# One decoder step on one core: the expert loop turned so that both branches come before the scatter, numbering after the second branch, placing ahead of the second token turn, activation turns as transposes

## The chip, the cores and the metric

The kernel runs on one core of a Trainium2 chip. The metric is device time in microseconds (us), the median of three runs. Durations and times within the program come from one profiled execution. An operand is always float32 unless said otherwise.

## The reference

One inference step of a one-layer decoder trunk for 256 prompt tokens and 32 sample tokens, 288 in all, of width 2048: a mixing block, cross-attention, and a hierarchical mixture of experts, which is where the change lies. For the normed tokens `t` it computes

```python
p_g = softmax(t @ wg + bg); g_sel = argmax(p_g)            # one of 4 groups
e_sel = (t @ we + be) of that group                        # 4 experts in it
top_p, top_i = top_k(softmax(e_sel), 2)
wts = top_p / sum(top_p) * p_g[g_sel]
act = silu(t @ w_gate[e]) * (t @ w_up[e]) * gate           # per chosen expert, d_ff = 512
out = act @ w_down[e]
x = x + out;  y = rmsnorm(x, norm_final)
```

There are 16 experts, each with w_gate and w_up of 2048 x 512 and w_down of 512 x 2048.

## The kernel before, in words

The engines run programs of their own and meet by semaphores: PE multiplies, ACT (ScalarE), DVE (VectorE) and POOL (GpSimd) do the rest, and SP issues the loads. The program is written out by hand, so the order in the code is the order on each engine. PE's results lie in PSUM in eight banks of 512 columns.

**Work of the expert stage.** A job is one expert with up to C = 64 tokens, its slots. Jobs go in pairs, and `n_loops` pairs run in a loop that all engines have, with one pair more behind it. The trace has eight pairs: seven turns and the last. Each pair takes 24 weight tiles of 1 MB (2048 columns on 128 partitions), numbered from `TILE["moe"]`: 0 to 7 gate and up of the first job, 8 to 15 gate and up of the second, 16 to 23 down of both. For the loop's own numbers 24 to 39 are the branches of the next pair. They go through 14 slots (`moe_slot`), and SP issues them in that order (`moe_load`, L596 to L612), each when PE has released the tile that lay in its slot: tiles 14 to 23 lie where 2 to 11 of the same pair lay, and 26 to 35 where 14 to 23 lay; slots 0, 1, 12 and 13 are used once in a pair. An issue that waits holds back all behind it.

**Work of a pair on PE.** `pair` (L1194) begins when the first job's branch is done:
- `place` (L1176): six small products and turns from `pick` (which token sits in which slot), for the gates and the matrix `spread` that takes slots back to tokens;
- `turn_act` (L1184): the activated branch of job 0 is turned, as four products with the identity;
- `branch(1, 8, ...)` (L1162): job 1's gate and up products, four groups of two tiles each, into one bank, `BRANCH_BANK`. Behind its first group stands `number_slots` (L1153), which works out the slots of the next pair;
- a second `turn_act`, which waits for ACT's silu (L1537) and DVE's product (L2133) of that branch;
- the down products (L1220) into banks 4 to 7, four groups of two tiles;
- ACT and DVE copy the result, scaled, to `y_pair` (L1552, L2146); then the scatter (L1230), 16 products of `y_pair` with `spread` in four steps of four, each of which DVE adds to the residual `xT` (L2152);
- in a loop turn `branch(0, 24, ...)`: job 0's branch of the next pair, behind the last addition.

POOL gathers the tokens of the next pair into `xe` (`gather`, L739): job 0's slots once their numbers are there and PE is through with the old ones, then job 1's. DVE makes the next pair's `pick` (`make_picks`, L2106).

**Ahead of the loop.** The routing works on all 288 tokens in three chunks: 128, 128 and the 32 of the sample. PE turns the normed tokens to rows (L1103), ACT scales them (`tokens_out`, L1486), PE turns them back (`turn_back`, L1112), ACT copies them to `h_moe` (L1496, L1500). Behind all three turns, PE counts for every token its place in its expert's queue (L1146), DVE makes `pick` from it (L2066 to L2074), and PE numbers the slots (L1157); ACT copies these (L1517). Then POOL gathers the first 32 slots of each job of pair 0, and ACT the other 32 (L1527), and PE starts `branch(0, 0, None)`, the first of 64 rows at L1170. Only then does the loop come.

Of the kernel before, what the change touches and what calls it, by code (L numbers as in the profile page):

```python
# [13 lines left out]
P = 128  # L14
D = 2048
DB = D // P
TP = 256
# [43 lines left out]
PE_EVENTS, MOE_SLOTS = 7, 14  # L61
HC = C // 2
NX = NJ - NE
# [17 lines left out]
for _n, _c in (("x", 1), ("pack", 1), ("h", 3), ("x_rest", 2), ("mem", 2), ("gates", 4), ("mix_stat", 2),  # L81
               ("states", 1), ("xattn_stat", 2), ("router", 1), ("h_tok", 1), ("logits", 1), ("h_tok_rest", 2),
               ("h_moe", 3), ("places", 1), ("counts", 1), ("pick_0", 1), ("moe", 6), ("final_sum", 1), ("y_0", 1), ("final_stat", 1), ("y_rest", 2)):
# [51 lines left out]
def build(nc, a, o):  # L135
    ctx = ExitStack()
    with ctx:
# [26 lines left out]
        expert_of = sb("expert_of", [1, NJ], I32)  # L164
# [5 lines left out]
        def cut(at, *shape):  # L170
# [55 lines left out]
        job_first, at = cut(at, NJ)  # L226
# [85 lines left out]
        xe_ready, xe_second_half = sem("xe_ready"), sem("xe_second_half")  # L312
        h_tok_out, h_moe_out, root_loaded = sem("h_tok_out"), sem("h_moe_out"), sem("root_loaded")
        place_out, act_out, product_out, low_banks_out, high_banks_out = map(
            sem, ("place_out", "act_out", "product_out", "low_banks_out", "high_banks_out"))
# [126 lines left out]
        slot_sums = ps[0:1, 7, 3 * P:3 * P + 2 * C]  # L442
        place_sums = lambda c: bank(UNIT["places"], 1 + c // 2)[:, c % 2 * P:c % 2 * P + NE]
        first_slot_sums = ps[0:1, 4 * ((UNIT["places"] + 1) % 2) + 3, 0:2 * C]
# [209 lines left out]
        def _(pool):  # L654
# [84 lines left out]
            def gather(p, s, slots):  # L739

                for first in range(0, slots, 16):
                    at = C * s + first
                    for n, token in enumerate(tokens_of_slots(mybir.EngineType.Pool, p, at, 16)):
                        m = nc.gpsimd.tensor_copy(xe[:, :, at + n:at + n + 1], h_moe_or_zero[:, :, bass.ds(token, 1)])  # L744
# [5 lines left out]
            for s in range(2):  # L750
                gather(0, s, HC)
# [11 lines left out]
        def _(pe):  # L763
# [369 lines left out]
            for c in range(2):  # L1133
                start_unit(pe, UNIT["h_moe"] + c)
                turn_back(c, lambda b: bank(UNIT["h_moe"] + c, b // 4)[:, b % 4 * P:(b % 4 + 1) * P])
# [24 lines left out]
            ACT_BANK, BRANCH_BANK, GATE_BANK, SPREAD_BANK = 4, 5, 6, 7  # L1160

            def branch(s, t, i, groups=range(4)):  # L1162

                for g in groups:
                    wait_moe_tile(pe, t + 2 * g, i)
                    wait_moe_tile(pe, t + 2 * g + 1, i)
                    for k in range(KT):
                        b = KT * g + k
                        for n in range(2):
                            m = mm(ps[C * n:C * n + C, BRANCH_BANK, :], xe[:, b, C * s:C * s + C],  # L1170
# [4 lines left out]
            def place():  # L1175

                for c in range(3):
                    n = own_rows[c]
                    mm(ps[:, GATE_BANK, 0:2], pick[0:n, c, :], job_gate[0:n, c, :], start=(c == 0), stop=(c == 2))
                for c in range(3):  # L1180
                    n = own_rows[c]
                    nc.tensor.transpose(ps[:, SPREAD_BANK, c * P:c * P + n], pick[0:n, c, :], ident[0:n, 0:n])
# [8 lines left out]
            def scatter_bank(q):  # L1191

                return 4 * ((q + 1) % 2)

            def pair(i, last):

                place()
                pe.wait_ge(product_out, plus(1, i, 2))
                turn_act()
                pe.wait_ge(xe_ready, plus(2, i, 2))  # L1200
                branch(1, 8, i, range(1))
                if not last:
                    pe.wait_ge(pick_ready, plus(2, i, 1))
                    pe.wait_ge(place_out, plus(1, i, 1))
                    number_slots(slot_sums)
                branch(1, 8, i, range(1, 4))
                pe.wait_ge(product_out, plus(2, i, 2))
                pe.wait_ge(act_out, plus(1, i, 2))
                turn_act()

                if not last:
                    pe.wait_ge(slots_out, plus(2, i, 1))
                pe.wait_ge(act_out, plus(2, i, 2))
                pe.wait_ge(place_out, plus(1, i, 1))
                for k in range(KT):
                    for s in range(2):
                        wait_moe_tile(pe, 16 + 2 * k + s, i)
                    for b in range(4):
                        for s in range(2):
                            m = mm(ps[C * s:C * s + C, 4 + b, :], actT[:, s, k, :],  # L1220
                                   moe_tile(16 + 2 * k + s)[:, b * TW:(b + 1) * TW], start=(k == 0), stop=(k == KT - 1))
                    m.then_inc(tile_used, 2)
                for q in range(4):
                    if q % 2 == 0:
                        pe.wait_ge(high_banks_out, plus(2 + q // 2, i, 4))
                    elif q == 3:
                        pe.wait_ge(low_banks_out, plus(1, i, 2))
                    for b in range(4):
                        j = 4 * q + b
                        m = mm(ps[:, scatter_bank(q) + b, 0:T], y_pair[:, j * P:(j + 1) * P], spread[:, :],  # L1230
                               start=True, stop=True)
                    m.then_inc(unit_done, 1)
                if not last:
                    pe.wait_ge(low_banks_out, plus(2, i, 2))
                    pe.wait_ge(high_banks_out, plus(4, i, 4))
                    pe.wait_ge(xe_ready, plus(3, i, 2))
                    branch(0, 24, i)
# [975 lines left out]
```

## Time and profile before

| | |
|---|---|
| median of three runs | 1531.19 us |
| the three runs | 1523.59, 1531.19, 1532.20 us |
| profiled execution, its own time | 1530.45 us |
| its span | 1528.7 us |
| granted TensorE clock, mean | 0.978 of full |
| PE busy | 1431.7 us, 94% of the span |
| DVE, ACT, POOL busy | 36%, 12%, 52% |
| bytes by DMA | 377.07 MB, 247 GB/s mean |

The span runs from the first to the last instruction; the execution's own time is 1.75 us longer. Busy PE time holds pipelined products whose ends are modelled. A clock of 1.00 in a stretch is 2.4 GHz, 0.50 is 1.2 GHz. A float32 product shows as two PE rows, so that the 32 products of one group of two tiles, at 512 columns and two at a time, are 16 rows in the chain.

### The profile page before, as it was taken

How to read it: one execution, taken by the hardware profiler on the slowest of the kernel's cores; microseconds unless marked ns; L12 is line 12 of the kernel's file. 1: busy time of each engine (PE TensorE's matmuls, PEld its weight loads, DVE VectorE, ACT ScalarE, POOL GpSimd, SP SyncE). 2: the span in 40 equal slices, each digit the busy share in tenths (PEclk: the TensorE clock that was granted, in tenths of full speed). 3: DMA queues.
4: the chain of work that ended last, by engine and by line, in shares of the span. 5: the costliest groups of instructions: out<-in, count | busy, mean ns of one | idle time of the engine just before them, and what ended most of it. 6: DMA issues, size and time to landing. Idle time of an engine off the chain costs nothing.

```text
span 1528.7 us, 25461 instructions
## 1 busy us (share of the span) xinstructions
PE 1431.7 (94%) x9302; PEld 1113.5 (73%) x9302; DVE 555.8 (36%) x1018; ACT 187.6 (12%) x390; POOL 797.3 (52%) x1461
## 2 busy tenths in 40 slices
PE   7999999999989999999999899979989999899997
PEld 6999999998879999987777699943443434434434
DVE  3546578749573423112111631231211112212104
ACT  4101321000000010013222100060000000000002
POOL 3777598879967757753453547324053151340500
PEclk8999999999999999999999899979999999999999
DMA  7344344445544444555879434829999999999991
GB/s 248 121 155 145 103 138 142 161 162 182 179 153 158 156 146 140 218 194 189 306 305 359 140 111 165 327 114 384 420 414 417 404 423 404 422 404 403 422 371 62
DMA packets 106121, 377.07 MB, mean 247 GB/s; under 512 B 12422, under 2 KB 12422, under 8 KB 76291
## 3 DMA queue, kind: packets, MB, share of 16 engines
q1 hardware_dynamic: 103778, 371.68, 64.3%
q10 hardware_dynamic: 2272, 4.42, 0.8%
q8 instruction: 48, 0.79, 0.2%
q14 instruction: 23, 0.18, 0.0%
HBM read 369.30 MB, written 6.77 MB: 246 GB/s over the span
## 4 chain that ended last, share of the span: by engine, by line
PE 89%; DVE 5%; ACT 2%; issue 1%; DMA 1%; SPq 0%; POOL 0%; POOLq 0%; ACTq 0%; DVEq 0%
PE ps L835 39%; PE ps L1170 15%; PE ps L892 13%; PE ps L1220 8%; PE ps L1230 4%; PE ps L960 2%; PE ps L785 1%; PE ps L1187 1%; PE ps L978 1%; DVE xT L2152 1%; PE ps L968 1%; PE ps L1026 1%; DVE A L2146 1%; PE ps L999 0%; DMA A<-in_norm_final 0%
## 5 line engine op out<-in xcount | busy, mean ns | idle before, releaser
L835 PE MATMUL ps<-hT,tiles 128*128 128x144 f32 x1792 | 295.3, 288 | 8.2 <-ACT kv_stage L1397 3.2
L744 POOL COPY A<-A 128x16 f32 x960 | 146.6, 212 | 299.5 <-issue 299.5
L835 PE MATMUL ps<-A,tiles 128*128 128x144 f32 x1792 | 265.2, 288 | 5.8 <-DVE mT L1643 3.9
L835 PEld LDWEIGHTS ps<-hT,tiles 128*128 128x128 f32 x1792 | 251.5, 191 | 9.9 <-ACT kv_stage L1397 3.5
L835 PEld LDWEIGHTS ps<-A,tiles 128*128 128x128 f32 x1792 | 239.9, 192 | 6.9 <-issue 4.7
L699 POOL TENSOR_TENSOR tiles<-tiles 128x512 f32<-128x512 f32 x88 | 117.4, 1334 | 192.1 <-DMA tiles<-in_w_in 70.2
L835 PE MATMUL ps<-tiles 128*128 128x144 f32 x960 | 170.9, 287 | 0.0
L1170 PE MATMUL ps<-tiles,A 128*64 128x512 f32 x512 | 146.8, 606 | 20.1 <-DVE xT L2152 12.7
L835 PEld LDWEIGHTS ps<-tiles 128*128 128x128 f32 x960 | 140.2, 191 | 0.0
L892 PE MATMUL ps<-tiles,mT 128*128 128x256 f32 x512 | 132.8, 382 | 4.1 <-ACT kv_stage L1397 4.1
L1662 DVE COPY pair_sums<-ps 128x144 f32<-128x144 f32 x44 | 13.5, 308 | 312.5 <-PE ps L835 312.5
L704 POOL TENSOR_TENSOR tiles<-tiles 128x512 f32<-128x512 f32 x88 | 119.1, 1354 | 6.9
L702 POOL TENSOR_TENSOR tiles<-tiles 128x512 f32<-128x512 f32 x88 | 121.7, 1383 | 0.0
L701 POOL TENSOR_TENSOR tiles<-tiles 128x512 f32<-128x512 f32 x88 | 117.6, 1336 | 6.9
L1220 PE MATMUL ps<-tiles,mT 128*64 128x512 f32 x448 | 120.1, 614 | 0.0
L892 PEld LDWEIGHTS ps<-tiles,mT 128*128 128x128 f32 x512 | 93.6, 190 | 23.0 <-ACT kv_stage L1397 6.8
L1170 PEld LDWEIGHTS ps<-tiles,A 128*64 128x64 f32 x512 | 45.6, 139 | 85.1 <-issue 84.6
L892 PE MATMUL ps<-tiles,A 128*128 128x256 f32 x384 | 103.8, 379 | 0.0
L689 POOL TENSOR_TENSOR tiles<-tiles 128x512 f32<-128x512 f32 x32 | 45.4, 1418 | 100.6 <-DMA tiles<-in_xa_w_v 90.6
L2133 DVE TENSOR_TENSOR mT<-mT,ps 64x512 f32<-64x512 f32 x16 | 11.0, 690 | 228.4 <-ACT mT L1537 228.4
L1170 PE MATMUL ps<-A 128*64 128x512 f32 x320 | 87.2, 599 | 0.0
L892 PEld LDWEIGHTS ps<-tiles,A 128*128 128x128 f32 x384 | 73.0, 190 | 9.9
(341 smaller groups left out, 1708.1 us busy)
## 6 DMA issues: line engine op xcount, KB each, us to landing
tiles<-in_expert_w_down SPq DMA_DIRECT2D x56, 1024.0 KB, 8.6
tiles<-in_w_in SPq DMA_DIRECT2D x40, 1024.0 KB, 5.1
tiles<-in_expert_w_gate SPq DMA_DIRECT2D x32, 1024.0 KB, 11.1
tiles<-in_expert_w_up SPq DMA_DIRECT2D x32, 1024.0 KB, 12.0
A<-in_expert_w_up SPq DMA_DIRECT2D x24, 1024.0 KB, 12.5
tiles<-in_xa_w_k SPq DMA_DIRECT2D x16, 1024.0 KB, 5.1
tiles<-in_w_out SPq DMA_DIRECT2D x16, 1024.0 KB, 5.1
tiles<-in_xa_w_q SPq DMA_DIRECT2D x16, 1024.0 KB, 5.0
```

Source lines behind the costliest of these rows:

```text
L689: step.tick(tt(t1, b12, b11, ALU.subtract))
L699: step.tick(tt(s1, a21, a22, ALU.add))
L701: tt(a21, a11, a21, ALU.subtract)
L702: step.tick(tt(s2, s1, a11, ALU.subtract))
L704: tt(s4, a12, s2, ALU.subtract).then_inc(weights_summed, 1)
L744: m = nc.gpsimd.tensor_copy(xe[:, :, at + n:at + n + 1], h_moe_or_zero[:, :, bass.ds(token, 1)])
L835: return mm(one(u + mp, x, TH), w[:, kp, mp, :], rhs, start=(first and g == 0 and kp == 0), stop=(g == 3 and kp == 1), skip_group_check=True)
L892: return mm(one(u, x, TW // 2), own, w[:, kp, :], start=(first and g == 0 and kp == 0), stop=(g == 3 and kp == 1), skip_group_check=True)
L960: m = nc.tensor.transpose(attention_bank(i % 2)[:, b * P:(b + 1) * P], cache_tile(tile)[:, (4 * (i % 4) + b) * P:(4 * (i % 4) + b + 1) * P ...
L1170: m = mm(ps[C * n:C * n + C, BRANCH_BANK, :], xe[:, b, C * s:C * s + C], moe_tile(t + 2 * g + n).rearrange("p (k n) -> p k n", k=KT)[:, k, :],
L1220: m = mm(ps[C * s:C * s + C, 4 + b, :], actT[:, s, k, :], moe_tile(16 + 2 * k + s)[:, b * TW:(b + 1) * TW], start=(k == 0), stop=(k == KT ...
L1230: m = mm(ps[:, scatter_bank(q) + b, 0:T], y_pair[:, j * P:(j + 1) * P], spread[:, :], start=True, stop=True)
```

## The change

On PE the loop is turned. Ahead of it now stand the whole first pair of branches; a turn is `down(i)`, `branch(0, 24, i)` and `second_branch(32, 4, i, True)`: `place`, branch 1 of the next pair, and behind that branch the numbering of the pair after it and the scatter of pair i. The scatter is eight steps of two products, each added by DVE on its own, in two alternating pairs of banks; four steps stand ahead of the second activation turn and four behind it. The two branches get banks of their own (4 and 5), down uses banks 0 to 3, and the activation turn bank 7. `make_picks` runs one pair further ahead, so the tables `expert_of` and `job_first` have two entries more. Three of the four products of an activation turn become transposes.

Ahead of the loop the places are worked out behind the first turn back, and DVE computes the gates after `pick` and no longer before. The first gather is split 24 : 24 : 16 between POOL, ACT and DVE, for job 0; job 1 keeps 32 : 32.

In the diff, cut to what the text speaks of:

```diff
-               ("values", 8), ("heads", 2), ("w_o", 8), ("router", 1), ("h_tok", 3), ("h_moe", 2),
-               ("places", 1), ("final_stat", 1), ("y", 3)):
+               ("values", 8), ("heads", 2), ("w_o", 8), ("router", 1), ("h_tok", 3), ("h_moe", 1),
+               ("places", 1), ("h_moe_rest", 1), ("final_stat", 1), ("y", 3)):
...
-            for s in range(2):
-                gather(0, s, HC)
+            gather(0, 0, POOL_SLOTS)
+            gather(0, 1, HC)
...
+            turn_back_chunk(0, UNIT["h_moe"])
             u = UNIT["places"]
             start_unit(pe, u)
-            turn_back(2, lambda b: bank(u, 0)[:, b * NB * ST:(b + 1) * NB * ST])
...
             def turn_act():
 
                 for k in range(KT):
-                    m = mm(ps[:, ACT_BANK, k * C:(k + 1) * C], act_nat[0:C, k * P:(k + 1) * P], ident[0:C, 0:C],
-                           start=True, stop=True)
+                    dst, own = ps[:, ACT_BANK, k * C:(k + 1) * C], act_nat[0:C, k * P:(k + 1) * P]
+                    if k == 0:
+                        mm(dst, own, ident[0:C, 0:C], start=True, stop=True)
+                    else:
+                        m = nc.tensor.transpose(dst, own, ident[0:C, 0:C])
                 m.then_inc(unit_done, 1)
...
+            def scatter(u, i):
+
+                if u < 2:
+                    pe.wait_ge((y_low_out, y_high_out)[u], plus(1, i, 1))
+                    pe.wait_ge(place_out, plus(1, i, 1))
+                else:
+                    pe.wait_ge(residual_added, plus(8 + u - 1, i, 8))
+                for n in range(2):
+                    j = 2 * u + n
+                    m = mm(ps[:, 2 * (u % 2) + n, 0:T], y_pair[:, j * P:(j + 1) * P], spread[:, :], start=True, stop=True)
+                m.then_inc(unit_done, 1)
+
+            def second_branch(t, n, i, scattered):
+
+                pe.wait_ge(xe_ready, plus(n, i, 2))
                 place()
+                branch(1, t, i, range(1))
+                pe.wait_ge(product_out, plus(n - 1, i, 2))
+                turn_act()
+                branch(1, t, i, range(1, 4))
+                pe.wait_ge(pick_ready, plus(n // 2 + 1, i, 1))
+                number_slots(slot_sums)
+                if scattered:
+                    for u in range(4):
+                        scatter(u, i)
+                pe.wait_ge(product_out, plus(n, i, 2))
+                pe.wait_ge(act_out, plus(n - 1, i, 2))
+                turn_act()
+                if scattered:
+                    for u in range(4, 8):
+                        scatter(u, i)
...
+            second_branch(8, 2, None, False)
             with pe.Fori(0, n_loops) as i:
-                pair(i, False)
-            pair(n_loops, True)
+                down(i)
+                pe.wait_ge(xe_ready, plus(3, i, 2))
+                branch(0, 24, i)
+                pe.wait_ge(place_out, plus(1, i, 1))
+                second_branch(32, 4, i, True)
+            down(n_loops)
...
             with dve.Fori(0, n_loops) as i:
                 step.enter(i, 2)
-                pair(i, False)
+                e = EVENT["moe"]
+                upper_y(i)
+                product(24, 0, 3, i)
+                turned_act(0, e, i)
+                make_picks(i + 2)
+                product(32, 1, 4, i)
+                for u in range(4):
+                    add_scattered(u, e + 2 + u, i)
+                turned_act(1, e + 6, i)
+                for u in range(4, 8):
+                    add_scattered(u, e + 3 + u, i)
```

How this moves the instructions is shown at three places. The names in the rows are tiles in SBUF and PSUM: `ps` is PSUM, `A` holds `xe`, `y_pair`, `pick` and some weight tiles, `mT` the activations, and `tiles`, `kv_stage` and `hT` hold weight tiles. A name behind "waits" is a semaphore.

PE in the loop, from the end of the second job's branch to the down products (L1220), in the kernel before:

```order
L1170 MATMUL ps<-A 64x512 [waits moe_loaded3,moe_loaded2]
L1170 MATMUL ps<-A 64x512 x7
L1187 MATMUL ps<-ident,mT 128x64 [waits act_out,product_out]
L1187 MATMUL ps<-ident,mT 128x64 x3
L1220 MATMUL ps<-kv_stage,mT 64x512 [waits moe_loaded4,place_out,moe_loaded5,act_out,slots_out]
```

The same place now, where L1160 is the numbering, L1206 the scatter and L1192 with L1194 the activation turn:

```order
L1173 MATMUL ps<-A 64x512 x7
L1217 REGISTER_ALU
L1160 MATMUL ps<-A 1x128 [waits pick_ready]
L1160 MATMUL ps<-A 1x128 x2
L1206 MATMUL ps<-A 128x288 [waits place_out,y_low_out]
L1206 MATMUL ps<-A 128x288
L1206 MATMUL ps<-A 128x288 [waits place_out,y_high_out]
L1206 MATMUL ps<-A 128x288
L1203 REGISTER_ALU
L1206 MATMUL ps<-A 128x288 [waits residual_added]
L1206 MATMUL ps<-A 128x288
L1203 REGISTER_ALU
```

The second activation turn stood directly behind the branch whose product it waits for; now the numbering and four scatter steps stand between the two, and four steps more behind the turn.

PE in the loop, from the end of the down products to the next pair's first branch, before:

```order
L1220 MATMUL ps<-tiles,mT 64x512 x7
L1225 ISA
L1230 MATMUL ps<-A 128x288 [waits high_banks_out]
L1230 MATMUL ps<-A 128x288 x7
L1225 REGISTER_ALU
L1230 MATMUL ps<-A 128x288 [waits high_banks_out]
L1230 MATMUL ps<-A 128x288 x3
L1230 MATMUL ps<-A 128x288 [waits low_banks_out]
L1230 MATMUL ps<-A 128x288 x3
L1235 REGISTER_ALU [waits low_banks_out]
L1236 REGISTER_ALU [waits high_banks_out]
L440 REGISTER_ALU [waits xe_ready]
```

And now, with the down products at L1239 and the branch at L1173:

```order
L1239 MATMUL ps<-tiles,mT 64x512 x7
L1261 REGISTER_ALU
L442 ISA [waits xe_ready]
L1173 MATMUL ps<-tiles,A 64x512 [waits moe_loaded1,moe_loaded0]
L1173 MATMUL ps<-A 64x512
```

The branch no longer stands behind the copies to `y_pair`, the scatter and the additions; it waits for the gathered tokens and its tiles alone.

ACT ahead of the loop, from the last `tokens_out` to the copy of the slot numbers, before:

```order
L1486 ACTIVATE mT<-ps,mT 32x2048 [waits unit_done]
L1496 COPY A<-ps 128x16x128 [waits half0_free,unit_done]
L1496 COPY A<-ps 128x16x128 [waits half1_free,unit_done]
L1500 COPY A<-ps 128x16x32 [waits half0_free,unit_done]
L1517 CAST tiles<-ps 1x128 [waits unit_done]
```

And now, with `tokens_out` at L1510, the turned-back chunks at L1517 and L1539, the exponentials at L1533 and the slot numbers at L1525:

```order
L1510 ACTIVATE mT<-ps,mT 32x2048 [waits half1_free,unit_done]
L1517 COPY A<-ps 128x16x128 [waits half0_free,unit_done]
L1533 ACT_TABLE_LOAD [waits half1_free]
L1533 ACTIVATE mT<-mT 128x3x4 [waits gate_in]
L1534 ACTIVATE mT<-mT 128x3
L1517 COPY A<-ps 128x16x128 [waits unit_done]
L1525 CAST tiles<-ps 1x128 [waits half1_free,unit_done]
L1539 COPY A<-ps 128x16x32 [waits unit_done]
```

The slot numbers stand ahead of the sample's copy instead of behind it, and the exponentials between the two chunks.

## Rows read from the trace of the kernel before

**Rows 1.** The page: GB/s moved, in 40 equal slices of the span

```profile
GB/s 248 121 155 145 103 138 142 161 162 182 179 153 158 156 146 140 218 194 189 306 305 359 140 111 165 327 114 384 420 414 417 404 423 404 422 404 403 422 371 62
```

**Rows 2.** The chain that ended last, one pair: start, us, engine, line, count

```profile
1243.03 15.66 PE ps L1220 x64
...
1258.72 1.29 DVE A L2146
...
1260.06 8.04 PE ps L1230 x32
1268.13 1.36 DVE xT L2152
...
1269.91 13.95 PE ps L1170 x64
1283.86 0.85 PE ps L1179 x6
1284.71 0.54 PE ps L1182 x3
1285.27 1.10 PE ps L1187 x8
1286.37 3.58 PE ps L1170 x16
1289.95 0.83 PE ps L1157 x6
1290.79 10.47 PE ps L1170 x48
1301.28 0.60 ACT mT L1537
...
1301.91 0.70 DVE mT L2133
...
1304.32 15.66 PE ps L1220 x64
```

**Rows 3.** The same chain: down products of the second and of the last pair

```profile
1122.17 13.97 PE ps L1220 x64
...
1487.36 13.97 PE ps L1220 x64
```

**Rows 4.** Windows: busy us by engine, then PEclk, DMA share, GB/s

```profile
1243.00:1244.50 1.50, 1.47 (x4) 0.53 (x6) 0.00 (x0) 0.00 (x0) 1.17 (x8) 0.58 1.01 421
...
1206.90:1208.60 1.70, 0.00 (x0) 0.00 (x1) 1.30 (x1) 0.00 (x0) 0.00 (x0) 1.00 1.02 424
```

**Rows 5.** Windows of the weight stream, same columns

```profile
1100.00:1152.00 52.00, 46.81 (x214) 21.55 (x215) 10.89 (x19) 3.26 (x7) 19.56 (x128) 0.97 1.00 417
...
1221.00:1273.00 52.00, 46.81 (x215) 21.43 (x213) 10.88 (x19) 3.26 (x7) 19.54 (x128) 0.97 1.01 423
...
1275.00:1282.00 7.00, 7.00 (x36) 2.82 (x34) 0.00 (x0) 0.00 (x0) 0.00 (x0) 1.00 0.84 316
```

**Rows 6.** SP's issue of the fifteenth tile, and its time to landing

```profile
1033.69 0.35 SPq L612 DMA_DIRECT2D A<-in_expert_w_gate  x1
...
A<-in_expert_w_gate SPq DMA_DIRECT2D x1, 1024.0 KB, 4.9
```

**Rows 7.** Timeline ahead of the loop: PE, ACT, ACT, POOL, PE

```profile
1009.01 1.97 PE L1112 MATMUL ps<-ident,A 128*128 128x128 f32 x16 [0.21 <-ACT mT L1486]
...
1011.17 1.87 ACT L1496 COPY A<-ps 128x2048 f32<-128x2048 f32 x1 [0.17 <-ACT A L1496]
...
1017.40 0.26 ACT L1517 CAST tiles<-ps 1x128 int32<-1x128 f32 x1 [3.66 <-PE ps L1157]
...
1019.21 2.43 POOL L744 COPY A<-A 128x16 f32 x16 [26.79 <-issue]
...
1024.71 1.08 PE L1170 MATMUL ps<-tiles,A 128*64 128x512 f32 x1 [7.34 <-POOL A L744]
```

**Rows 8.** Timeline of DVE in an earlier stage: an addition of 576 columns

```profile
963.45 0.76 DVE L1878 TENSOR_TENSOR xT<-xT,ps 128x576 f32<-128x576 f32 x1
```

More of the change, by code:

```diff
@@ L58 @@
 NSTATE = S_SC + (1 + NB) * (SW - 1)
-PE_EVENTS, MOE_SLOTS = 7, 14
+PE_EVENTS, MOE_SLOTS = 11, 14
 HC = C // 2
+POOL_SLOTS, ACT_SLOTS = 24, 48
 NX = NJ - NE
@@ L1218, in pair @@
                     for b in range(4):
+                        if k == 0 and b % 2 == 0:
+                            pe.wait_ge(residual_added, plus(8 - 1 + b // 2, i, 8))
                         for s in range(2):
-                            m = mm(ps[C * s:C * s + C, 4 + b, :], actT[:, s, k, :],
+                            m = mm(ps[C * s:C * s + C, b, :], actT[:, s, k, :],
                                    moe_tile(16 + 2 * k + s)[:, b * TW:(b + 1) * TW], start=(k == 0), stop=(k == KT - 1))
                     m.then_inc(tile_used, 2)
[L1223 to L1237, printed above, removed]
-            read_out(pe, UNIT["h_moe"] + 1)
+            turn_back_chunk(1, UNIT["h_moe_rest"])
             pe.wait_ge(tokens_numbered, 1)
@@ L1539, in pair, with place_read @@
-            def pair(i, last):
-                e = EVENT["moe"]
+                fn(silu[0:C, :], ps[0:C, 4 + s, :], ACT.Silu).then_inc(silu_ready, 1)
+            def place_read(e, i):
                 after_event(act, e, i, PE_EVENTS)
                 for s in range(2):
-                    copy(place_gate[C * s:C * s + C, 0:1], ps[C * s:C * s + C, 6, s:s + 1])
-                copy(spread[:, :], ps[:, 7, 0:T]).then_inc(place_out, 1)
-                if not last:
-                    slots_numbered(slot_sums, e + 1, i, i + 1)
-                gate_branch(8, i)
+                    copy(place_gate[C * s:C * s + C, 0:1], ps[C * s:C * s + C, 6, T + s:T + s + 1])
+                copy(spread[:, :], ps[:, 6, 0:T]).then_inc(place_out, 1)
@@ L1549, in pair, with lower_y @@
+            def lower_y(i):
                 after_tile(act, TILE["moe"] + 16 + 7, i, 24)
                 act.wait_ge(place_out, plus(1, i, 1))
-                dst, src = lower(y_pair, 4)
-                fn(dst, src, ACT.Copy, scale=place_gate[:, 0:1]).then_inc(high_banks_out, 1)
-                if not last:
-                    gate_branch(24, i)
-            gate_branch(0, None)
+                dst, src = lower(y_pair, 0)
+                fn(dst, src, ACT.Copy, scale=place_gate[:, 0:1]).then_inc(y_low_out, 1)
@@ L2047, in _ @@
             m.then_inc(mask_ready, 1)
+            dve.wait_ge(consts_set, 10)
+            u = UNIT["places"]
+            after_event(dve, EVENT["places"])
+            for c in range(3):
+                m = stt(out=posm[:, c, :], in0=place_sums(c), scalar=4.0 * NOWHERE, in1=mask16[:, c, :],
+                        op0=ALU.add, op1=ALU.mult)
+            then(m)
+            then(ts(posm[:, :, :], posm[:, :, :], -4.0 * NOWHERE, None, ALU.add))
+            for g in range(2):
+                for c in range(3):
+                    m = ts(pick[:, c, C * g:C * g + C], place_iota[:, 0, :], posm[:, c, g:g + 1], None, ALU.is_equal)
+            m.then_inc(pick_ready, 1)
+            after_event(dve, EVENT["counts"])
+            v.tensor_copy(tab[:, 0, :], bank(u, 3)[:, 0:NE]).then_inc(half_free[u % 2], 2)
+            dve.wait_ge(gate_exp, 2)
             then(v.tensor_reduce(G(18, 1), G(4), AX.X, ALU.add))
@@ L2059, in _ @@
             then(m)
-            dve.wait_ge(consts_set, 10)
-            u = UNIT["places"]
-            after_event(dve, EVENT["places"])
-            for c in range(3):
-                m = stt(out=posm[:, c, :], in0=place_sums(c), scalar=4.0 * NOWHERE, in1=mask16[:, c, :],
-                        op0=ALU.add, op1=ALU.mult)
-            then(m)
-            then(ts(posm[:, :, :], posm[:, :, :], -4.0 * NOWHERE, None, ALU.add))
             dve.wait_ge(root_loaded, 1)
@@ new lines, in _ @@
+            step.leave_dynamic(n_loops)
+            upper_y(n_loops)
+            for q in range(4):
+                after_event(dve, EVENT["scatter"] + q, n_loops, PE_EVENTS)
+                first = 4 * ((q + 1) % 2)
+                x = xT[:, 4 * q:4 * q + 4, :]
+                tt(x, x, ps[:, first:first + 4, 0:T], ALU.add).then_inc(last_added, 1)
+                dve.wait_ge(last_added, q + 1)
+                for b in range(4 * q, 4 * q + 4):
+                    m = ts(hT[:, b, :], xT[:, b, :], gain("norm_final", b), None, ALU.mult)
+                m.then_inc(h_ready, 1)
```

201 lines of the change are left out of this document (96 added, 105 removed).

## The prediction

> **What bounds the kernel now.** I read the page's slices first. From the 29th to the 38th they move 403 to 423 GB/s; ahead of that the rate changes from slice to slice [rows 1]. That is the expert stage, which streams its weights. Then the chain that ended last, for one pair. From one start of the down products to the next are 1304.32 - 1243.03 = 61.29 us, and almost all of it is PE: down 15.66, scatter 8.04, first branch 13.95, `place` 0.85 + 0.54, activation turn 1.10 (there are two), second branch 3.58 + 10.47, numbering 0.83 [rows 2]. Between these PE stands still for others: 1.29 for the copy to `y_pair`, 1.36 for the last addition to `xT`, 0.60 + 0.70 for silu and product, and some 1.5 in hand-offs that the rows leave as gaps. So PE is the bound by the chain.
>
> The down products take 15.66 us here and 13.97 in the second and the last pair [rows 2, 3]. The difference, 1.69, is clock: just behind the wait for the product and the short turn, the window from 1243.00 shows 0.58, which is a mixture of 1.2 and 2.4 GHz. But a wait alone didn't do it: the 1.70 us from 1206.90, in which PE is idle after the scatter's last step, stand at 1.00 [rows 4]. The row with 15.66 comes five times, and in one more turn the same time is lost in the first group of the second branch; so six of the seven turns of the loop take 61.3 us, counted between the ends of the down products.
>
> Then the windows of the stream, which decide the case. Over 52 us it moves 423 GB/s in one pair and 417 in an early one; only in the 7 us around 1278 does it fall to 316 [rows 5]. That is a hole of (423 - 316) / 423 x 7 = 1.8 us. A pair's 24 tiles are 24 x 1.0486 = 25.17 MB; at 422, between the two rows and nearer to the one that repeats, they take 59.6 us, 2.485 a tile. 59.6 + 1.8 is the 61.3 of the pair. So the stream is only 1.7 us faster than PE, and the hole is its own waiting for a slot: whoever takes more than 1.7 us a pair from PE makes the stream the bound.
>
> **The change in the loop, PE's side.** PE's work in a turn is down 13.97 at full clock, first branch 13.95, `place` 1.39, second branch 14.05, numbering 0.83, scatter 8.04: 52.2 [rows 2, 3]. Two turns come to it. Three transposes in `place` are three instructions (0.54 x3), where the activation turn's four products are eight, 0.14 each [rows 2]. With one product and three transposes five are left, 0.7 a turn. Bounds: 0.55, if only four issue slots count, and the old 1.10. With 0.6 for hand-offs, PE needs 54.2 us.
>
> The waits go as follows. The copy to `y_pair` (1.29) lies beside the first branch, which now has banks of its own. Silu and product of the first branch (1.3) lie beside `place` and the second branch's first group (5.0). Those of the second lie beside numbering and two scatter steps, 0.83 + 2.0. What is late next there is the first addition: DVE has it behind the product, at 1.4 us after the branch, while scatter step 0 ends at 1.8, so the product doesn't delay it. Each scatter step is 8.04 / 8 = 1.0 us of PE; an addition of 576 columns took 0.76 [rows 8], and step u + 2 waits for addition u with step u + 1 between: 0.8 under 1.0, hidden. POOL's gather now runs beside these additions. If it slowed them to what twice the columns take, 1.36 [rows 2], the chain would be DVE's, 8 x 0.4 = 3 us longer. I take 0, since POOL was at work beside the 0.76 too.
>
> The gather of the next pair starts at the numbering, not in the middle of the branch. 64 slots are four times 2.86 us (2.43 and the loading of 16 numbers), 11.4 us [rows 7]. From the numbering to the next first branch are 9.6 + 13.97 = 23.6 us, so 12 us of cover are left; every us beyond it would stand on PE. The order in which SP issues is the same, no queue gets another DMA, and the two new entries of the tables change no tile.
>
> **The stream's side.** 54.2 is 5.4 below 59.6, so PE catches up and then waits for tiles: 3.49 us of work in a group against 4.97 for its two tiles. From there each pair costs 59.6, not 54.2. Does the stream get a new hole? Tile 26 goes where tile 14 lay. In the first pair PE is through with 14 at some 1054, and the stream reaches 26 at 1063; later, PE uses each tile as it lands, and even behind the scatter's 9.9 us pause only four of 14 slots have filled. I count no hole. Gain: 61.3 - 59.6 = 1.7 in each of six loop turns, 10 us, out of 7.1 that PE saves in each.
>
> **Ahead of the loop.** Before, ACT copied the second chunk until 1013.04, and the slot numbers were out at 1017.66, since places, `pick` and numbering came behind it; ACT idled 3.66 in it [rows 7]. Now these lie beside the chunks. In return the second chunk can be turned only when ACT has emptied the first, near 1011, so PE's 1.97 no longer overlaps: 1013.0, numbering 1013.9, the copy until 1014.9, slot numbers 1015.2, and the sample's copy, with a quarter of the columns 0.5 to 0.6, until 1015.9. With PE at half clock it is 1017. The exponentials, which now stand between the two chunks on ACT, lie beside PE's turn. I take 1016.4, 1.3 earlier. POOL then gathers 24 slots instead of 32 ahead of PE's start: 8 x 2.43 / 16 = 1.2. DVE's 16 copies of the same kind are not in the trace; between 0 and POOL's 2.43 for 16 they are done before POOL's 24, but their numbers must be loaded first, as POOL's were (1.55 from 1017.66 to 1019.21), by an engine that has the gates to finish. Sum 2.5, bounds 0 and 3.5.
>
> **The sum.** The fifteenth tile is issued at 1033.69, when the first branch has freed its slot, and lands 4.9 later, at 1038.6 [rows 6]. Now 2.5 earlier: 1036.1. 177 further tiles at 2.485 land until 1475.9. The last second branch has its tiles eight earlier, at 1456.0. Behind them PE has 3.5 for the group, 0.83, 8.04, 0.7 and 0.3 of hand-offs: 1469.4. Down adds 13.97, its tiles being there: 1483.3. Before it was 1487.36 + 13.97 = 1501.3 [rows 3]: 18 us, made of 2.5 ahead, 10 in the loop and 5.5 in the last pair, where PE is again alone. The end, 1528.7 - 1501.3 = 27.4, is kept in its old form. That gives a span of 1510.7 and, with the 1.75 around it, 1512. The profiled execution had 1530.45 and the median is 1531.19, so the same sum from there ends within 1 us.
>
> **Two rules of the Trainium skill.** PE will idle 1.5 us per group, which no row shows in this rhythm. The Trainium skill, "TensorE: Matmul & The Clock Gate", section "HAM oscillation — how this bites in real kernels", tells of a kernel that waits for a DMA behind each batch of products and is thrown back to the low clock every time. By it each group would be colder, as the second rival has it; the row from 1206.90 speaks against it. And "DMA: Bandwidth & Descriptors" of the Trainium skill, section "Where 436 GB/s comes from", gives 435 GB/s as the ceiling of the fabric and warns of about 358 from HBM. This stream holds 423, so the trace contradicts the lower one. By the upper one a pair would take 57.8, an estimate from that page, and the time would be some 13 us less.
>
> **The rivals.** *The stream stays the bound* (1512): for it the flat 423, a row that comes alike in five turns, and a hole exactly as long as PE's excess. Chance 0.72, with a range of its own from 1506 to 1518.
>
> *PE's new order costs back its slack.* Four stretches at the low clock per turn, each 1.69, make 54.2 + 6.8 = 61.0, so PE is nearly as slow as before; up to three are hidden in the 5.4. Then seven turns cost 1.4 more each: 1522. For it: such a stretch came once in almost every pair. Against: it came where short turns and a wait fell together, and these are now apart. Chance 0.20.
>
> *PE is still the bound and the stream follows*: the first branch starts at 1022.2; it, with 1.69 at the low clock, `place`, the second branch, both turns, numbering, the wait for the product and down are 48.6 us, so the first down ends at 1070.8. With 7 x 54.2, 27.4 and 1.75 that is 1479. For it is only that PE fills the chain; no window of the stream shows the rate of 464 GB/s that it needs. Chance 0.03.
>
> *Slower.* The scatter becomes stop-and-go: if each of the eight steps waits for its own addition, 1.0 + 0.76 + 0.2, it takes 15.7 instead of 8.04, and with one low-clock stretch a turn is 54.2 + 7.7 + 1.7 = 63.6. 1070.8 + 7 x 63.6 + 29.1 is 1545. It decides from 61.5 us a turn on, where the time before is reached. Against it: two pairs of banks take turns. Chance 0.05.
>
> **How the numbers follow.** 1% is 15 us, about what can be told from no change here: faster ends at 1516, slower begins at 1546 with the median's scale. The first case lies below 1516 in all but 0.04, the third wholly: 0.71 faster. The second and most of the slower case's lower part are within: 0.24. 0.05 are left for slower, the stop-and-go and what is unforeseen. The range, 1502 to 1525, holds the first case with the rate's bounds (417 to 426 GB/s are +5 and -4), the start's (+2.5, -1) and an execution with fewer low-clock stretches in the 1000 us ahead, and reaches over most of the second.
>
> **What would show it.** In the profile after: 59.6 us from one down to the next; the stream at 422 with no hole and PE waiting for tiles at each group; no wait of PE for copies, product or addition over 0.3; the first branch from 1022; the last landing near 1476; the down products of the last pair over at 1483. Wrong would be: PE without waits for tiles in the loop, a granted clock well below 0.97 there, a hole in the stream, or the first branch still at 1024.

## The result and the profile after

The changed kernel takes 1512.76 us in the median of seven runs (1506.88 to 1517.16). Run again beside the variants below it took 1510.82 (1506.61 to 1513.20). The ratio to the kernel before is 0.9902 the first time, with a 95% interval of 0.9878 to 0.9926, and 0.9884 (0.9864 to 0.9905) the second. The kernel before had 1531.19 in three runs; in seven it has 1523.59, and in the larger sets of the experiments 1527.5 to 1528.5. The ratio on record is not the quotient of the two medians of seven, which is 0.993; against the medians of the larger sets it is 0.990. So the time came out as forecast (1512.0), and the gain is 1.0 to 1.2% by the ratios, where 1512.0 is 1.25% below 1531.19. Whether it lies above 1% is not settled by these intervals.

The page's slices of the changed kernel, first its span, then GB/s as in [rows 1]:

```profile
span 1512.4 us, 25461 instructions
...
GB/s 251 140 143 161 88 137 150 156 160 186 172 156 167 139 166 141 192 226 124 335 318 313 223 84 151 277 212 288 420 422 422 421 422 422 422 421 422 422 422 76
```

Before, the ten slices of the expert stage went up and down between 403 and 423. Now eleven stand at 420 to 422: in these slices the stream has no hole.

The chain that ended last, for one turn of the loop, with the columns of [rows 2]:

```profile
1163.15 0.83 PE ps L1160 x6
1163.98 4.22 PE ps L1206 x16
1168.20 0.36 PE ps L1192 x2
1168.56 0.19 PE ps L1194 x3
1168.75 4.22 PE ps L1206 x16
1172.97 13.88 PE ps L1239 x64
1186.86 6.89 PE ps L1173 x32
...
1194.45 24.55 DMA A<-in_expert_w_up
...
1219.14 3.65 PE ps L1173 x16
1222.79 0.83 PE ps L1160 x6
```

From numbering to numbering are 59.64 us, where a turn in [rows 2] took 61.29. No wait for a copy, an addition or a product is left between PE's pieces; the activation turn is 0.36 + 0.19 instead of 1.10. In the middle the chain leaves PE for a tile on its way: of the turn, 24.6 us belong to one DMA.

Who waits for whom, over 305 us of the loop of the changed kernel (engine, tile and line, what it waited for: us in total, times, longest):

```profile
DVE xT L2174 <- PE ps L1206: 14.5, 40, 0.7
PE ps L1173 <- DMA tiles<-in_expert_w_up: 13.2, 15, 1.3
PE ps L1173 <- DMA hT<-in_expert_w_up: 6.6, 5, 1.3
PE ps L1173 <- DMA A<-in_expert_w_up: 6.6, 5, 1.3
```

PE's waits are all for tiles, 25 in five turns, up to 1.3 us each: ahead of five of the eight groups that a turn's two branches have. DVE waits for PE's scatter at every addition, and no product waits for an addition (a weight load of the scatter does at times, by up to 0.3 us).

The window of the stream and SP's fifteenth tile, to be laid beside [rows 5] and [rows 6]:

```profile
1221.00:1273.00 52.00, 48.85 (x227) 20.09 (x223) 11.41 (x23) 3.26 (x7) 19.62 (x128) 1.00 1.01 422
...
1031.45 0.35 SPq L614 DMA_DIRECT2D A<-in_expert_w_gate  x1
```

The granted clock over these 52 us rose from 0.97 to 1.00, although PE now stops five times a turn for a tile.

Ahead of the loop, the timeline of ACT, PE, DVE, POOL and PE, as in [rows 7]:

```profile
999.22 1.97 ACT L1510 ACTIVATE A<-ps,mT 128x2048 f32<-128x2048 f32 x1 [0.57 <-DVE mT L2042]
...
1009.75 3.59 PE L1114 MATMUL ps<-ident,A 128*128 128x128 f32 x16
...
1015.42 0.26 ACT L1525 CAST tiles<-ps 1x128 int32<-1x128 f32 x1
...
1017.76 2.40 DVE L2103 COPY A<-A 128x16 f32 x16 [4.64 <-issue]
...
1017.68 3.64 POOL L746 COPY A<-A 128x16 f32 x24 [27.09 <-issue]
...
1021.63 1.08 PE L1173 MATMUL ps<-tiles,A 128*64 128x512 f32 x1 [6.33 <-POOL A L746]
```

The first row is the mark for all that follows: ACT scales the first chunk of tokens. In the profiled execution before, this came at 1001.06, here at 999.22, and none of the code ahead of it was changed. Executions differ by some us before they reach the stage of the change, so I count from this mark. To the first branch it was 23.65 us and is 22.41; to the end of the span it was 527.6 and is 513.2.

### The profile page after: what moved, and what is told of

Same layout as the page of the kernel before. It is cut to its first block and busy times, and to the rows that moved or that the text cites. A ratio compares the mean times of both kernels' runs of the same rounds, so it can differ in the third digit from the quotient of the medians.

```text
span 1512.4 us, 25461 instructions
## 1 busy us (share of the span) xinstructions
PE 1423.3 (94%) x9260; PEld 1092.9 (72%) x9260; DVE 565.7 (37%) x1074; ACT 186.9 (12%) x383; POOL 796.9 (53%) x1453
## 5 line engine op out<-in xcount | busy, mean ns | idle before, releaser
L1173 PE MATMUL ps<-tiles,A 128*64 128x512 f32 x512 | 147.7, 602 | 18.8 <-DMA tiles<-in_expert_w_up 12.5
L1239 PE MATMUL ps<-tiles,mT 128*64 128x512 f32 x448 | 113.3, 597 | 0.0
L894 PEld LDWEIGHTS ps<-tiles,mT 128*128 128x128 f32 x512 | 94.5, 192 | 23.4 <-ACT kv_stage L1421 6.8
L1173 PEld LDWEIGHTS ps<-tiles,A 128*64 128x64 f32 x512 | 45.8, 138 | 84.5 <-issue 84.1
L1173 PE MATMUL ps<-A 128*64 128x512 f32 x320 | 88.0, 602 | 8.8 <-DMA A<-in_expert_w_up 8.8
## 6 DMA issues: line engine op xcount, KB each, us to landing
tiles<-in_expert_w_down SPq DMA_DIRECT2D x56, 1024.0 KB, 23.4
```

The costliest lines, as they stand in the source:

```text
L894: return mm(one(u, x, TW // 2), own, w[:, kp, :], start=(first and g == 0 and kp == 0), stop=(g == 3 and kp == 1), skip_group_check=True)
L1173: m = mm(ps[C * n:C * n + C, BRANCH_BANK + s, :], xe[:, b, C * s:C * s + C], moe_tile(t + 2 * g + n).rearrange("p (k n) -> p k n", k=KT)[: ...
L1239: m = mm(ps[C * s:C * s + C, b, :], actT[:, s, k, :], moe_tile(16 + 2 * k + s)[:, b * TW:(b + 1) * TW], start=(k == 0), stop=(k == KT - 1))
```

## The experiments

Twelve more kernels ran (two of them repetitions), with the kernel before beside them. The marks of their profiled executions, all in us; the last column is the turns of the loop, counted from one end of the down products to the next:

| kernel | ratio to before (95%) | mark | mark to first branch | mark to end | turns |
|---|---|---|---|---|---|
| before | | 1001.06 | 23.65 | 527.6 | 61.3 x6, 58.8 |
| b_again | 1.0003 (0.9989 to 1.0018) | 994.47 | 23.37 | 530.4 | 59.6, 61.3 x5, 58.8 |
| b_half | 0.9996 (0.9981 to 1.0010) | 997.50 | 23.85 | 528.1 | 61.3 x6, 58.8 |
| b_turn | 0.9903 (0.9880 to 0.9927) | 996.98 | 23.37 | 515.9 | 58.6 x4, 60.3 x2, 57.8 |
| after | 0.9902 (0.9878 to 0.9926) | 999.22 | 22.41 | 513.2 | 54.5, 59.7 x6 |
| a_again | 0.9884 (0.9864 to 0.9905) | 995.64 | 20.73 | 511.4 | 54.4, 59.7 x6 |
| a_half | 0.9652 (0.9627 to 0.9677) | 998.10 | 22.05 | 474.2 | 53.4 x7 |
| a_noturn | 0.9895 (0.9874 to 0.9915) | 998.80 | 22.47 | 513.8 | 54.4, 59.6 x6 |
| a_front0 | 0.9898 (0.9879 to 0.9916) | 998.06 | 24.35 | 515.7 | 54.6, 59.7 x6 |
| a_split | 0.9894 (0.9874 to 0.9913) | 995.39 | 24.13 | 514.2 | 56.3, 59.7 x6 |
| a_place2 | 0.9908 (0.9883 to 0.9932) | 997.52 | 20.56 | 515.6 | 57.9 x2, then 59.7, 57.6 |
| a_place6 | 1.035 (1.032 to 1.038) | 996.57 | 22.25 | 585.0 | 66.1 to 69.0 |
| a_warm | 0.9880 (0.9860 to 0.9899) | 997.26 | 20.23 | 508.3 | 54.4, 59.7 x6 |
| a_warm_early | 0.9885 (0.9865 to 0.9906) | 1000.78 | 20.67 | 509.2 | 54.8, 59.7 x6 |

**The kernel before once more.** No edit. Its times spread over 10 us, and the forecast had to know whether that lies in the loop.

> The kernel before, unchanged, for a second profile. It has run between 1522 and 1532 us. Theory clock: a turn of the loop takes 61.3 us with one stretch at the low clock and 59.6 without, so an execution near 1523 has turns of 59.6 and no row of 15.66 at the down products, and the stream has no hole of 1.8 us left. Theory ahead: the 8 us lie ahead of the expert stage; the turns are 61.3 in every execution and the first branch starts earlier. Ratio to itself 1.00.

```profile
994.47 1.97 ACT L1486 ACTIVATE A<-ps,mT 128x2048 f32<-128x2048 f32 x1 [0.57 <-DVE mT L2020]
...
1118.30 13.97 PE ps L1220 x64
...
1179.59 13.97 PE ps L1220 x64
...
1361.75 15.66 PE ps L1220 x64
...
1423.03 15.66 PE ps L1220 x64
```

The first row is ACT's timeline, the others are from the execution's chain. The mark comes 6.6 us earlier than in the first profile, yet the loop is nearly the same: five turns take 61.3 us, also where the down products take 13.97 (from 1118.30 to 1179.59 are 61.29), since the low clock then falls on the second branch. The first takes 59.6, without such a stretch, and the last 58.8 as before. So the theory that a whole execution's loop runs at one of two speeds falls. But the execution as a whole is only 3.8 us shorter: of the 6.6 us, 4.4 are lost again between the mark and the end of the first down products, where more of the first pair lies at the low clock (first branch 17.0 us instead of 15.7, the group behind it 5.28 instead of 3.58, down 15.66 instead of 13.97), and the loop gives back 1.6. The spread has parts on both sides of the mark, the larger one ahead of it. What makes them was not pursued.

**Less stream, before and after.** In both kernels only half the columns of each w_down tile are loaded; the other half keeps old data, so these two kernels compute something else.

```diff
-                sp.dma_start(moe_tile(m), src).then_inc(moe_loaded[moe_slot(m)], 16)
+                sp.dma_start(moe_tile(m)[:, 0:n], src).then_inc(moe_loaded[moe_slot(m)], 16)
...
-                    moe_load(m + j, e_down[bass.ds(experts[j % 2], 1), :, j // 2].rearrange("o p m -> (o p) m"), i)
+                    moe_load(m + j, e_down[bass.ds(experts[j % 2], 1), :, j // 2, 0:D // 2].rearrange("o p m -> (o p) m"), i, D // 2)
```

> The kernel before; of each w_down tile only the first half of the columns is loaded, the rest is left as it lies (part of the down products is computed from old data). A pair's stream falls from 25.2 to 21.0 MB, 49.7 us. If PE bounds the kernel before, its turns stay 59.6 to 61.3 us and the time falls by under 3 us. If the stream bounds it already, the turns get shorter and the time falls by more than 5.

> The changed kernel with the same halved w_down loads. Theory stream: the turns fall from 59.65 to PE's own 54.2 us, 7 x 5.4 less, and the time to some 1476 us; PE shows no wait for tiles. Rival, hand-offs and clock bound the changed loop: the turns stay above 58 us and the time above 1500.

Before, nothing moves: 0.9996, turns of 61.3. After, the ratio falls to 0.9652, 1474.52 us. The chain of one turn of a_half:

```profile
1110.58 13.88 PE ps L1239 x64
1124.46 13.73 PE ps L1173 x64
...
1143.72 10.45 PE ps L1173 x48
...
1155.00 4.22 PE ps L1206 x16
...
1159.77 4.22 PE ps L1206 x16
...
1164.00 13.88 PE ps L1239 x64
```

1164.00 - 1110.58 is 53.42 us, PE without a wait. That is what the change made of PE's 61.3 (1.7 of it a stretch at the low clock, which is gone too), and 59.65 is what the stream lets through. Of 7.9 us saved per turn, 6.2 are invisible.

**The transposes alone, in the kernel before.**

```diff
-                    m = mm(ps[:, ACT_BANK, k * C:(k + 1) * C], act_nat[0:C, k * P:(k + 1) * P], ident[0:C, 0:C],
-                           start=True, stop=True)
+                    dst, own = ps[:, ACT_BANK, k * C:(k + 1) * C], act_nat[0:C, k * P:(k + 1) * P]
+                    if k == 0:
+                        mm(dst, own, ident[0:C, 0:C], start=True, stop=True)
+                    else:
+                        m = nc.tensor.transpose(dst, own, ident[0:C, 0:C])
```

> The kernel before with nothing but the transposes of the change: three of the four products of each activation turn. PE saves 2 x 0.55 = 1.1 us a pair of the 1.7 that the stream leaves it: 8 x 1.1, so about 8 us less, in turns of 60.2 with a low-clock stretch. In turns of 59.6 without such a stretch there is nothing to gain but the last pair and the time falls by 1 to 3 us.

This was the surprise. Six instructions fewer in a pair, and the ratio is 0.9903, that of the whole change; the median is 1513.32, where some 8 us less than before was expected and 14 were measured. Its down products in the chain:

```profile
1175.80 15.66 PE ps L1223 x64
...
1236.13 13.97 PE ps L1223 x64
...
1294.76 13.97 PE ps L1223 x64
...
1353.39 15.66 PE ps L1223 x64
```

A turn without a low-clock stretch is 58.63 (1294.76 to 1353.39) where it was 59.59, the 1.0 that was expected; eight of those are 8 us. The rest, some 6 us, is mostly that of the seven turns counted only two have such a stretch in full (60.3), where before it was six (61.3): four times 1.7. The mean of the seven is 59.0 us, and the stream stands at 422 from 1100 to the end of the loads, with no wait of PE for a tile from 1080 to 1460: PE and the stream run level there. That the mean can lie below the stream's 59.65 since the loop begins with tiles in hand is my reading; no run tests it. Why a turn that is 1 us shorter meets the low clock less often, no run of mine separates.

**The changed kernel without its transposes.** The same lines the other way round, with the changed kernel unchanged beside it.

> The changed kernel, unchanged, beside the variants of this call. Ratio 0.990 to the kernel before, turns of 59.65 us, waits for tiles of 1.3 us at each group of the branches. The start of the router's part may move by some us from one execution to the next.

> The changed kernel with all four products of each activation turn as before. Theory stream: PE's 1.1 us more a pair lie in its slack of 5; turns stay 59.65 and only the last pair and the first show it, 1 us more at most. Rival, the transposes carry the whole gain, as they did when put into the kernel before alone (0.9903): the time goes back to the one of the kernel before.

0.9895 against 0.9884, turns of 59.6 as before, and 513.8 from mark to end against 513.2 and 511.4. The rival falls: the transposes are worth 14 us in one kernel and at most 2, within the noise, in the other. The turned loop without them reaches the same bound as they do without the turned loop. The two gains don't add.

**The stage ahead of the loop undone**, places behind all turns back, the gates ahead of `pick` and the gather 32 : 32, then the gather alone. The lines, cut to the main ones:

```diff
             turn_back_chunk(0, UNIT["h_moe"])
+            turn_back_chunk(1, UNIT["h_moe"] + 1)
             u = UNIT["places"]
             start_unit(pe, u)
+            turn_back(2, lambda b: bank(u, 0)[:, b * NB * ST:(b + 1) * NB * ST])
...
-POOL_SLOTS, ACT_SLOTS = 24, 48
+POOL_SLOTS, ACT_SLOTS = 32, 64
```

> The changed kernel with everything ahead of the loop as before: places behind all three turns back, gates ahead of pick, the first gather 32 : 32. The loop stays turned. Theory stream: the stream restarts when the first branch has freed its slots, so what the front gives goes through to the end in full. By the prediction that is 2.5 us; by the two traces, counted from the first scaled chunk to the first branch (23.65 against 22.41), 1.2 us. Turns stay 59.65.

> The changed kernel with the first gather back at 32 slots on POOL and 32 on ACT, nothing on DVE. By the prediction the split gives 1.2 us (8 copies of 0.15 on POOL). By the trace of the changed kernel POOL's 24 took 3.6 us with a break for loading and the first branch waited for it, so 1 to 1.5 us more; if DVE's copies beside POOL's slow these, less.

The turns don't change. From mark to first branch are 24.35 with all undone and 24.13 with the gather undone, against 20.56 to 22.47 in the six kernels that have the whole front of the change and no products ahead of the branch (after, a_again, a_half, a_noturn, a_place2, a_place6; their mean is 21.7). The four profiles of the old front in the old loop (before, b_again, b_half, b_turn) have 23.37 to 23.85, with a mean of 23.6. The ratios, 0.9898 and 0.9894 against 0.9884, overlap. So the traces give 1.9 us against the kernel before, 2.6 against a_front0 and 2.4 against a_split, and the timing can't confirm them.

Much of this spread arises in one place. Just behind the mark PE turns the normed tokens to rows, and the same 32 instructions take more or less time from one execution to the next:

```profile
999.48 5.36 PE L1105 MATMUL ps<-ident,hT 128*128 128x128 f32 x32 [1.13 <-DVE mT L2042]
...
1003.19 1.97 ACT L1510 ACTIVATE A<-ps,mT 128x2048 f32<-128x2048 f32 x1 [2.00 <-PE ps L1105]
...
995.90 3.71 PE L1105 MATMUL ps<-ident,hT 128*128 128x128 f32 x32 [1.13 <-DVE mT L2042]
```

The first two rows are from the changed kernel, where the granted clock over the 5.36 us is 0.68; the third is a_again, where it is 1.00. Where they take 3.71, mark to first branch is 20.6 and 20.7 with the new front (a_place2, a_again) and 23.4 with the old (b_again, b_turn): 2.7 us. Where they take 5.36 to 5.38 it is 22.4 and 22.5 (after, a_noturn) against 23.85 (b_half): 1.4 us; and a_split's 24.13 is 1.7 above the same two. In the kernel before, ACT has the exponentials to do in the meantime, so a low clock there costs it little; now ACT waits for PE, 2.00 us in the changed kernel. a_front0 had 6.64 us there (clock 0.54), which no other profile has, so the part of the places alone can't be read from it.

**How much slack PE has.** `place` is issued three and seven times:

```diff
-                place()
+                for _ in range(3):
+                    place()
```

> The changed kernel with the six small instructions of place issued three times instead of once, 2.8 us more PE work in each turn (the result is the same). Theory stream: PE's own turn is 53.4 us by the run with halved loads, 56.2 with this, under the 59.65 of the stream: turns stay 59.65, the time rises by under 1.5 us against the changed kernel (ratio 0.989 to 0.991). If clock and hand-offs had eaten the slack, 7 x 2.8 = 20 us come on top.

> The same with seven times place: 8.3 us more PE work in each turn, 61.7 against 59.65. Theory stream: the slack of 6.2 is used up, the turns become 61.7 us and PE waits for no tile; against the changed kernel about 7 x 2.1 + 5 = 20 us more, near 1530, as slow as the kernel before. If the slack is larger or smaller than 6.2, the turns show it.

With 2.8 us more, the first two turns take 57.9, PE's own pace (53.4 + 2.8 + 1.7, there is one low-clock stretch in each), and from where PE has caught up they are 59.7, except for the last with 57.6, which I leave unexplained. Ratio 0.9908: hidden, as expected. With 8.3 us more they should have been 61.7 and are 66.1 to 69.0. The chain of a_place6 shows where the rest comes from:

```profile
1232.78 0.85 PE ps L1182 x6
...
1235.63 1.46 PE ps L1182 x6
...
1244.05 0.86 PE ps L1185 x3
1244.91 5.62 PE ps L1173 x16
...
1236.00:1244.50 8.50, 8.50 (x34) 6.95 (x34) 0.00 (x0) 0.00 (x0) 0.00 (x0) 0.50 1.01 422
```

The last row is a window with the columns of [rows 4]: PE busy for all of 8.50 us, the granted clock at 0.50. From the fourth repetition on, the same six instructions take 1.46 instead of 0.85 and the three 0.86 instead of 0.54, and the group behind them 5.62 instead of 3.58: PE is never idle there and yet falls to the lower clock. Four repetitions at the low clock cost 0.93 each and the group 2.0, 5.8 in all, which is what 61.7 lacks to the 67.6 of four of the turns; in the two of 66.1 the stretch begins about one repetition later. My number was wrong, because I priced small instructions at the high clock.

**A warm start.** While PE waits for the gather, it multiplies the identity with itself, 12 times; nothing reads the result. In the second variant it does so 14 times and one wait earlier.

```diff
             pe.wait_ge(h_moe_out, 3)
+            for _ in range(12):
+                mm(ps[:, 7, 0:P], ident[:, :], ident[:, :], start=True, stop=True)
             pe.wait_ge(xe_ready, 1)
```

> The changed kernel with twelve products of the identity with itself ahead of the first branch, while PE waits for the gather (5.1 us at the low clock; nothing reads them). The first branch takes 16.3 to 17.0 us in the traces so far instead of 13.95, since PE comes out of a pause. Theory: at full clock it frees its slots up to 2.5 us earlier, the stream restarts as much earlier, and the whole time falls by as much: ratio 0.987 to 0.989. Rival: the low clock stays, because the products are too few, or the fast branch is bounded otherwise: no change.

> The same with fourteen such products, issued about 1 us earlier, before PE waits for the last chunk's copy. If the clock needs the longer run, this one has the first branch at 13.95 where the twelve leave a part of it at the low clock. If they run past the end of the gather, up to 0.7 us is lost.

The first branch in the chain of the changed kernel, then the timelines of PE and SP in a_warm:

```profile
1021.63 16.49 PE ps L1173 x64
...
1012.42 4.35 PE L1252 MATMUL ps<-ident 128*128 128x128 f32 x24 [0.77 <-ACT A L1541]
...
1017.49 0.64 PE L1173 MATMUL ps<-tiles,A 128*64 128x512 f32 x1 [0.72 <-POOL A L746]
...
1024.78 0.35 SPq L614 DMA_DIRECT2D A<-in_expert_w_gate  x1
```

Its first product takes 0.64 where it took 1.08. In both variants the first branch is 13.95 long, where it was 16.49 in the changed kernel, and SP's next tile follows 7.3 us behind its start instead of 9.8. The two differ in clock and pause: in a_warm the products run at a mean granted clock of 0.64 and PE then waits 0.7 us, in a_warm_early they run at 1.00, PE then waits 2.8 us, and the clock stays at 1.00 in that wait. From mark to end are 508.3 and 509.2, the two shortest with full loads. In time that is 1508.42 and 1510.35 us, ratios of 0.9880 and 0.9885. By the traces the first branch is 2.5 us shorter, and from mark to end the two are 3.1 and 2.2 us below a_again, whose 32 instructions behind the mark take the same 3.71; by the timing they are not told apart from a_again's 0.9884.

## Why the prediction was right, and where not

**The bound.** Right, and the experiments show it from both sides: PE bounded the kernel before (b_half), the stream bounds the changed one (a_half, a_place2). 59.6 us a turn were forecast, 59.65 measured; the rate 422, no hole. The eleven full slices, 11 x 37.8 = 416 us, stand at 420 to 422. "DMA: Bandwidth & Descriptors" of the Trainium skill, section "Where 436 GB/s comes from", says that the HBM side, about 358 GB/s, binds a transfer between HBM and SBUF; these slices contradict it for this core, and its 435 is not reached either.

**PE's side.** 54.2 forecast, 53.42 in a_half. The hand-offs of 0.6 were too many: the copy, silu and both products lie beside other work as worked out. The activation turn is 0.55, the lower bound, not 0.7. The scatter is 2 x 4.22 = 8.44, not 8.04; what the 0.4 are, no run separates. The additions took 0.75 with POOL's gather beside them and no product waited for one, so the stop-and-go rival has nothing for it.

**What the prediction did not draw from its own sentence.** It said that whoever takes more than 1.7 us a pair from PE makes the stream the bound, and then assigned the 10 us to the turned loop. By that sentence a much smaller edit could do as well. b_turn comes to the same time, though its transposes take only 1.0 of the 1.7 from a pair; the rest came with fewer stretches at the low clock, which was not forecast and which no run explains. The step is right in size, but it is not the turned loop's alone: a_noturn has the loop without the transposes and b_turn the transposes without the loop, each gains what the whole change gains, and together they gain no more.

**The front.** Forecast 2.5, bounds 0 and 3.5. The pair of profiles before and after says 1.24; executions with the same clock just behind the mark say 1.4 (low) and 2.7 (full); the means say 1.9. So the gain lies within the bounds, and the 2.5 was too much for this pair. Of its two steps POOL's was right: from the slot numbers to the first branch are 5.95 us instead of 7.05, 1.1 where 1.2 was taken (24 copies in 3.64). The other, slot numbers 1.3 earlier, gave 0.14 in the profile after (16.46 us behind the mark, before 16.60). Two things held it back: ACT's second chunk now waits for PE, which was at a clock of 0.68 there, and the turn back of that chunk, now behind PE's counts, took 3.59 at a clock of 0.53, where the sum had 1.97 and kept the low clock as its late case.

**The sum.** The span was forecast as 1510.7 with the mark where it was before. The profiled execution had 1512.4 with its mark 1.84 earlier, so from the mark it is 3.5 us over. 1.3 of this is the front in that one profile. 0.8 is the first branch, which the sum took over from the trace before: 12 of its rows instead of 8 ran at the low clock, and SP's fifteenth tile came 9.82 us behind its start instead of 8.98. From that tile to the end of the last down products 452.1 were forecast and 453.7 measured (453.6 in a_again): 1.3 lies in the stream before its last second branch, 0.3 in PE behind it. The end was 27.3, where 27.4 was kept. That the median met 1512.0 within 1 us is in part luck: these 3.5 us were made up by a start 1.8 us earlier and by a median 1.4 us below the profiled execution.

**The size of the gain.** The forecast set its time against the median of three runs, 1531.19. With more runs that kernel's median is 1523.6 to 1528.5, since its executions spread over 10 us (the marks of four profiles lie between 994.5 and 1001.1, and from mark to end are 527.6 to 530.4 in the three with its old times). So 1.25% became 1.0 to 1.2, at the edge of what was called faster.

**The clock.** The rival of a clock that eats the slack didn't come in the changed kernel: it waits for tiles 25 times in five turns and is at 1.00. The rule of the Trainium skill that I weighed, "TensorE: Matmul & The Clock Gate", section "HAM oscillation — how this bites in real kernels", tells of a kernel whose waits for DMA throw the clock back each time. Those waits are longer than the ones here; with waits of up to 1.3 us between dense groups of 3.65 this trace shows no such thing, and so it neither confirms nor contradicts the section. What cost clock in these runs was something else: a_place6 lost some 6 us a turn to the low clock without any wait.

## What to carry to other kernels

Before pricing what an edit takes off the busiest engine, work out how far the next bound is: here the stream of weights was 1.7 us a turn behind PE, so of the 7.9 us saved in a full turn 1.7 were the gain, and the other 6.2 were invisible. To see which resource binds, take work away from the one that you suspect and leave the rest, as the halved loads did in both kernels. And compare traces from a mark shortly ahead of the change: the larger part of the difference between two executions lay before it (6.6 us against 2.8 in the kernel before).

## What the runs showed that I had not expected

PE can fall to 1.2 GHz while it is busy all the time: in a_place6 the products with two columns and the transposes of `place` took 2.32 us a round instead of 1.39 from the fourth round on, and the dense group behind them 5.62 instead of 3.58. Waits of 1.3 us between dense groups did not do that. And 4.35 us of products that nobody reads, in a pause of 6 us, brought the branch behind them from 16.5 to 13.95 us; in a_warm_early the clock was still at 1.00 after 2.8 us in which PE did nothing, where a pause of 6.3 us in the changed kernel ended at 0.50.
